# Scaling the attention's probabilities on GpSimd instead of VectorE

## What is computed

```python
q = rmsnorm(q, q_g); k = rmsnorm(k, k_g)          # per head
q = axial_rope(q, rope); k = axial_rope(k, rope)
s = jnp.einsum('bqhgd,bkhd->bhgqk', qblk, k) * scale
p = jax.nn.softmax(s, axis=-1)
o = jnp.einsum('bhgqk,bkhd->bqhgd', p, v)
return o.reshape(B, S, 1024) @ w_o
```

## Time and profile before

| | |
|---|---|
| median of 3 runs | 935.67 us (935.48 to 935.76) |
| the profiled execution's own time | 936.85 us |
| its span, first to last instruction | 935.0 us |
| mean granted TensorE clock | 0.994 |
| TensorE busy | 907.0 us, 97% |
| DVE busy | 613.3 us, 66% |
| ScalarE busy | 497.1 us, 53% |
| attention, in the span | about 375 to 446 us |

### The profile page before, as it was taken

One profiled execution on the slowest core, in us unless ns is written; L12 is line 12 of the kernel. 1 busy time (PEld: TensorE's weight loads), 2 busy tenths in 40 slices (PEclk: granted clock), 3 DMA queues, 4 the chain that ended last, 5 costly groups with the idle time before them and its releaser, 6 DMA issues.

```text
span 935.0 us, 17321 instructions
## 1 busy us (share of the span) xinstructions
PE 907.0 (97%) x7189; PEld 839.9 (90%) x7189; DVE 613.3 (66%) x958; ACT 497.1 (53%) x729; POOL 0.2 (0%) x4
## 2 busy tenths in 40 slices
PE   5899999999999999999999999999999999999997
PEld 2688788899999999778999999998999999988886
DVE  0565685786776776787765555576886765566664
ACT  4537674754555567665644343346656653344333
POOL 0000000000000000000000000000000000000000
PEclk9899999999999999999999999999999999999999
DMA  9988757675556569415366565555442655555541
GB/s 351 369 292 275 271 182 249 211 254 204 171 175 218 180 169 179 105 46 163 109 216 195 195 195 196 179 181 180 128 143 95 222 176 172 188 186 181 181 135 45
DMA packets 130697, 176.78 MB, mean 189 GB/s; under 512 B 19696, under 2 KB 108188, under 8 KB 130620
## 3 DMA queue, kind: packets, MB, share of 16 engines
q1 hardware_dynamic: 129852, 173.51, 57.0%
q10 hardware_dynamic: 768, 2.16, 0.7%
HBM read 174.62 MB, written 1.05 MB: 188 GB/s over the span
## 4 chain that ended last, share of the span: by engine, by line
PE 84%; DVE 7%; ACT 4%; DMA 3%; issue 2%; SPq 0%; ACTq 0%; DVEq 0%
PE psum L1605 25%; PE psum L1597 21%; PE psum L1598 21%; PE psum L1601 4%; PE psum L1602 4%; DMA raw<-in_w_ada_dram 2%; DVE w_lo L956 2%; PE psum L1699 1%; ACT w_hi L526 1%; PE psum L2199 1%; PE psum L2154 1%; PE psum L2143 1%; PE psum L2133 1%; DMA raw<-in_w_in_dram 1%; DVE h_lo L994 1%
## 5 line engine op out<-in xcount | busy, mean ns | idle before, releaser
L526 ACT ACTIVATE w_hi<-raw 128x2048 fp32r<-128x2048 f32 (+1 forms) x139 | 264.5, 1905 | 147.4 <-PE psum L1605 122.1
L1597 PE MATMUL psum<-h_hi,w_hi 128*128 128x256 f32 x1352 | 328.7, 283 | 1.5 <-DVE h_lo L1128 1.1
L956 DVE TENSOR_TENSOR w_lo<-raw,w_hi 128x2048 fp32r<-128x2048 f32 (+1 forms) x139 | 313.2, 2278 | 22.2 <-ACT w_hi L526 22.1
L1598 PE MATMUL psum<-h_lo,w_hi 128*128 128x256 f32 x1352 | 324.5, 279 | 0.0
L1597 PEld LDWEIGHTS psum<-h_hi,w_hi 128*128 128x128 f32 x1352 | 254.4, 188 | 10.2 <-issue 7.2
L1598 PEld LDWEIGHTS psum<-h_lo,w_hi 128*128 128x128 f32 x1352 | 254.8, 188 | 0.8
L1605 PE MATMUL psum<-h_hi,w_lo 128*128 128x256 f32 x1352 | 186.9, 280 | 0.7 <-DVE w_lo L956 0.5
L1605 PEld LDWEIGHTS psum<-h_hi,w_lo 128*128 128x128 f32 x1352 | 170.3, 188 | 1.5 <-DVE w_lo L956 1.4
L1324 DVE SCALAR_TENSOR_TENSOR arena<-psum,rstd 128x256 f32<-128x256 f32 x64 | 26.9, 424 | 131.9 <-PE psum L1605 130.0
L1597 PE MATMUL psum<-a_hi,w_hi 128*128 128x256 f32 x464 | 110.6, 280 | 0.6 <-DVE a_lo L1311 0.4
L1598 PE MATMUL psum<-a_lo,w_hi 128*128 128x256 f32 x464 | 110.2, 279 | 0.0
(11 more groups left out here) (272 smaller groups left out, 899.3 us busy)
## 6 DMA issues: line engine op xcount, KB each, us to landing
raw<-in_mlp_w_in_dram SPq DMA_DIRECT2D x32, 1024.0 KB, 5.6
raw<-in_mlp_w_out_dram SPq DMA_DIRECT2D x32, 1024.0 KB, 7.1
raw<-in_w_ada_dram SPq DMA_DIRECT2D x24, 1024.0 KB, 7.6
raw<-in_w_up_dram SPq DMA_DIRECT2D x22, 1024.0 KB, 5.1
raw<-in_gla_w_in_dram SPq DMA_DIRECT2D x12, 1024.0 KB, 5.3
raw<-in_w_down_dram SPq DMA_DIRECT2D x11, 1024.0 KB, 5.4
raw<-in_w_in_dram SPq DMA_DIRECT2D x10, 1024.0 KB, 7.5
raw<-in_w_out_dram SPq DMA_DIRECT2D x4, 1024.0 KB, 5.9
```

Of the source, the lines that this page charges most:

```text
L526: act.activation(halved(w_hi, m % SPLIT_SLOTS, SPLITS[m]), halved(raw, r % RAW_SLOTS, SPLITS[m]), ACT.Copy).then_inc(*mark("w_hi", m))
L956: dve.tensor_tensor(halved(w_lo, m % SPLIT_SLOTS, key), halved(raw, r % RAW_SLOTS, key), halved(w_hi, m % SPLIT_SLOTS, key).bitcast(F32), ...
L1597: pe.matmul(dst, high, both[0], start=start, stop=False, skip_group_check=True)
L1598: return pe.matmul(dst, high, both[1], start=False, stop=False, skip_group_check=True)
```

## The change

The four multiplications of `att_scale(t)` leave DVE and are issued by GpSimd, which so far had no instructions of its own. DVE keeps the reciprocal and signals it. GpSimd waits for that signal, then scales the four pieces in the same order, and TensorE waits for them as before. From pair 2 DVE waits, ahead of the reciprocal, until GpSimd has scaled the last piece of pair t - 2, since the small tile with the reciprocals has two buffers.

```diff
             def att_scale(t):
                 dve.wait_ge(*at("act_read", "att", t, 1))
+                if t >= 2:
+                    dve.wait_ge(*at("att_scaled", t - 2, 1, 1))
                 dve.reciprocal(pair_small(t, 3), pair_small(t, 2)).then_inc(*mark("att_rden", t))
-                dve.wait_ge(*at("att_rden", t))
-                for n in range(2):
-                    for q in range(TT):
-                        pr = att_p[:, 2 * (t % 2) + n, q, :]
-                        dve.tensor_scalar(pr, pr, pair_small(t, 3)[:, TT * n + q:TT * n + q + 1], None, ALU.mult)\
-                            .then_inc(*mark("att_scaled", t, n, q))
...
+        @block.gpsimd
+        def _(pool):
+
+            def att_scale(t):
+                pool.wait_ge(*at("att_rden", t))
+                for n in range(2):
+                    for q in range(TT):
+                        pr = att_p[:, 2 * (t % 2) + n, q, :]
+                        pool.tensor_scalar(pr, pr, pair_small(t, 3)[:, TT * n + q:TT * n + q + 1], None, ALU.mult)\
+                            .then_inc(*mark("att_scaled", t, n, q))
+
+            for step in schedule():
+                if step[0] == "att_scale":
+                    att_scale(*step[1:])
```

## The result

| | before | after |
|---|---|---|
| median of 4 runs, us | 935.71 (935.48 to 935.76) | 953.81 (952.38 to 955.48) |
| ratio, 95% interval | | 1.0178 [1.0156, 1.0200] |
| profiled execution, us | 936.85, span 935.0 | 952.98, span 951.1 |

The changed kernel is slower by 18.1 us. The forecast had the side right and the size wrong: 942.3 us, with 947.5 as the upper end.

The account below looks back on a forecast made before the run. TensorE, busy 97% of the span, was taken as the bound. Delays of 0.5 + 0.4 + 1.1 + 2.8 + 1.8 = 6.6 us in pairs 0, 2, 3, 5 and 7 made 935.67 into 942.3 us, range 934.5 to 947.5.

Parts of the forecast that it names:

- At most 4.3 us can be won: Attention stretch: ceiling of any gain, 2.65 us of TensorE idle time plus 1.6 us of slow clock.
- I take 0.56 us: Price of one 128x256 GpSimd piece, from ScalarE's time for that shape; ends 0.349 and 0.691 us.
- Turns: GpSimd pieces and DVE instructions with two SBUF inputs each wait for the whole of the other; slower, 57%.
- Who yields: Pairs 0 and 2: pieces alternate with DVE's rotation instructions, delaying TensorE by 0.5 and 0.4 us.
- Pair 5: GpSimd finds L956 running behind the reciprocal, so its last piece comes late: 2.8 us, between 2.3 and 3.2.
- Pair 7: Four pieces plus one or two L1013 end after the transposes want them: 1.8 us.
- Pair 3: Late reciprocal and turns with the half-size rotation delay the last piece: 1.1 us more.
- Pairs 1, 4 and 6: Pairs whose scalings on GpSimd were to add no delay to TensorE: 0 us.
- The hop: Hand-over from DVE's reciprocal to GpSimd's first piece: 0.1 us, with 0.05 and 0.2 as ends.
- The new DVE wait: From pair 2, the reciprocal waits for the scaling two pairs back; costs nothing, reciprocals lying 12 to 14 us apart.
- The clock: TensorE's slow clock in the attention stays as before; another fall of 1.6 us kept only for the range.
- no turns, slow pieces: Rival, 10%: GpSimd pieces undisturbed but slow; 936.6 us at 691 ns each, 940.3 us at 1 us each.

Follow-up runs that it names:

- the narrow kernel: The changed kernel with each GpSimd piece cut to its first 112 of 256 columns, the rest left unscaled; 945.78 us, ratio 1.0085 to before.
- the reduction: The changed kernel with three L956, behind the reciprocals of pairs 0, 2 and 5, replaced by a one-input row maximum; 944.49 us, ratio 1.0073 to before.
- the filled kernel: The changed kernel with 20 unread 128x256 matmuls put into TensorE's waits in each of pairs 0 and 2; 954.47 us, ratio 1.0173 to before.
- the run of the free pieces: The kernel before with GpSimd scaling unused tiles of 64 to 1024 columns during the first MLP; 939.59 us in one run.

## Why the prediction was right in its side and wrong in its size

- **"At most 4.3 us can be won."** Overstated: 1.6 of it, the slow clock, covered a wait for ScalarE that showed once the clock held. Nor were the three idle times simply DVE's: the 0.87 us at 412 stayed at 0.85 with DVE freed, as ScalarE's rounding came first. Both counted only in the rivals and moved no number of the sum.
- **"I take 0.56 us"**, with 0.349 and 0.691 as ends: this is the step that failed. A piece takes 0.92 us undisturbed, above the upper end. ScalarE's row for the same shape was no guide to GpSimd's time, and neither was DVE's slowest row a bound for another engine. With pieces of 0.56 us the kernel gives a ratio of 1.0085 [1.0064, 1.0105], and the forecast was 1.0070. Two undisturbed pieces last 1.82 us and four 3.62 instead of 1.12 and 2.25. That the narrow kernel meets the forecast's total is in part luck: TensorE waits 2.8, 1.6, 0, 2.0 and 1.4 us for POOL in pairs 0, 2, 3, 5 and 7, where the sum had 0.5, 0.4, 1.1, 2.8 and 1.8.
- **Turns, 57%**: right. A piece that meets L956 lasts 3.02 us; with the reduction in its place it lasts 0.92. In a sentence apart: the Trainium skill (SBUF — State Buffer, "Who interferes with whom") says that a two-input DVE instruction and a reading GpSimd one exclude each other while a reduction leaves the port free. These runs agree for the GpSimd piece and for the reduction; that a piece under way blocks DVE they don't show, since the product at 384.49 starts inside a piece and keeps its 0.68 us.
- **Who yields**: in pairs 0 and 2 the forecast let pieces and rotation alternate and charged 0.5 and 0.4 us. DVE went through nearly without a pause and its L956 followed at once, so GpSimd lost each race: 3.25 and 2.85 us. Even with pieces of 0.56 us TensorE waits 2.81 in pair 0 and 1.63 in pair 2. "Each waiting for the whole of the other" was wrong for DVE. Pair 3, forecast at 1.1, cost nothing, since the wait in pair 2 had come first.
- **Pair 5, 2.8 us, "the largest term"**: 1.77 + 1.25 = 3.0 measured, by the mechanism named, GpSimd behind L956. **Pair 7, 1.8**: 2.9, four pieces of 0.92 us in place of 0.56 (1.4 us more). **Pairs 1, 4 and 6, 0**: 0.28, 0 and 0.
- **The hop, 0.1**: the reciprocal ends at 383.87, the first piece starts at 383.97. **The new DVE wait, 0**: no idle time of L1427 is put down to it. (The reciprocals of pairs 2 and 4 lie 10.6 us apart, closer than the "12 to 14" of the forecast, which changed nothing.)
- **The clock, kept at before's**: two falls instead of one, about 2.7 us more. The forecast's range held 3.2 for it, so the clock alone didn't take the time out of the range; the transposes run in two groups, about 1 us, were not in the sum at all.
- **The range** ended at 947.5 as it was built on 0.691 us. The rival "no turns, slow pieces" had looked at 1 us, and came to 940.3: the case that held, turns and 0.92 us together, was never worked out.

## What to carry to other kernels

Price an instruction on an engine that the trace doesn't show by rows of that engine, or leave the upper end open; here one-input GpSimd work costs 0.29 us and 2.5 ns a column, 2.6 times DVE's time at 256 columns. Then ask what the other engine runs right behind the step that is moved: a long instruction with two SBUF inputs there turns a 0.9 us piece into 3. And work moved off an engine that isn't the bound can win only the idle time which that engine causes on the bound, here under 3 us, while every hand-over it adds is charged to the chain.

## What the runs showed of the hardware that was not expected

- DVE, issuing back to back, keeps GpSimd out for several instructions (5.18 us behind two L957), whereas the longest L957 in that same stretch is 3.12 us against 2.28, beside pieces of 2.85 us. It doesn't always: another piece of the same width, below, started 0.33 us ahead of two L957 (477.91, the two together 4.68 us) and ended 0.7 behind the first. What decides is open.

```profile
477.58 3.32 POOL L1585 TENSOR_SCALAR arena<-arena,const 128x256 f32<-128x256 f32 x1
```

- One-input work isn't near line rate on GpSimd. In a sentence apart: the Trainium skill (GPSIMD Engine Reference, "4.1 Engine selection") calls it roughly that; here 1024 columns take 2.85 us on GpSimd, and DVE's own 256 take 0.349.
- The clock fell after idle times of 3.25 and 2.85 us, and not after 1.77 + 1.25 or 1.73 + 1.14 with matmuls between them; in the filled kernel, with 1.78 + 1.26 and 1.42 + 1.14, it fell at both places. Idle times of one length don't all act alike either: at 412 it fell at once behind 0.87 us of idle time in before and not behind 0.85 us with pairs 4 and 6 on GpSimd. In the run of the free pieces, whose attention is before's, it fell later and for longer, and the stretch took 68.08 us instead of 66.04. What decides is open.

```profile
415.00:420.00 5.00, 4.06 (x18) 2.94 (x17) 2.31 (x6) 3.25 (x12) 0.00 (x0) 0.50 0.00 0
```

- The first MLP has two paces for the same instructions. One step of it in the changed kernel, the same line at 485.08 and 496.38, takes 11.30 us, and in its repetition on another chip 11.20 (486.09 to 497.29):

```profile
485.08 0.42 DVE L1324 SCALAR_TENSOR_TENSOR arena<-psum,rstd 128x256 f32<-128x256 f32 x1 [1.31 <-PE psum L1617]
...
496.38 0.42 DVE L1324 SCALAR_TENSOR_TENSOR arena<-psum,rstd 128x256 f32<-128x256 f32 x1 [2.32 <-PE psum L1617]
```

Over most of the MLP's 16 steps that makes the 1.5 us of the account. The granted clock is 1.00 in both, and the narrow kernel's trace has the slow pace too (11.31 us a step). The same code shows both, so it isn't the change; its cause is open.
